# Two inverse square roots per round of an RWKV mixer, taken as exp(-ln/2) on ScalarE in place of a square root on ScalarE and a reciprocal on VectorE

## The reference, cut to what matters

```python
kk = hs(k * f('rwkv_k_k'))
kk = kk * lax.rsqrt(jnp.sum(kk * kk, axis=-1, keepdims=True) + 1e-12)
...
    decay = jnp.exp(-jnp.exp(w))
    a = jax.nn.sigmoid(f('rwkv_a0')[d] + xa @ f('rwkv_a_up')[d])
    yd, Sd = rwkv_scan(rh, hs(decay), kd, vh, kk, hs(a), s0[:, d], reverse=(d == 1))
...
y = ys[0] + ys[1]
mean = jnp.mean(y, axis=-1, keepdims=True)
var = jnp.mean(jnp.square(y - mean), axis=-1, keepdims=True)
yn = ((y - mean) * lax.rsqrt(var + GN_EPS)).reshape(b, n, D_RWKV) * f('rwkv_ln_g') + f('rwkv_ln_b')
out = (yn + (bonuses[0] + bonuses[1]).reshape(b, n, D_RWKV)) * g
```

## Time and profile before

| what | value |
|---|---|
| median of three runs | 3153.46 us (3147.15 to 3154.85) |
| the profiled execution | 3154.8 us |
| its span in the trace | 3153.0 us |
| busy: TensorE / weight loads | 2871.3 us (91%) / 2176.1 us (69%) |
| busy: VectorE / ScalarE / GpSimd | 1646.6 us (52%) / 1094.0 us (35%) / 165.9 us (5%) |
| mixer rounds, first layer | 364.2 to 688.3 us of the span |

### The profile page before, as it was taken

One profiled execution on the slowest core, in us unless ns is written; L12 is line 12 of the kernel. 1 busy time (PEld: TensorE's weight loads), 2 busy tenths in 40 slices (PEclk: granted clock), 3 DMA queues, 4 the chain that ended last, 5 costly groups with the idle time before them and its releaser, 6 DMA issues.

```text
span 3153.0 us, 48841 instructions
## 1 busy us (share of the span) xinstructions
PE 2871.3 (91%) x17315; PEld 2176.1 (69%) x17315; DVE 1646.6 (52%) x2172; ACT 1094.0 (35%) x1377; POOL 165.9 (5%) x209
## 2 busy tenths in 40 slices
PE   6899788889899999999878997888898999999997
PEld 1578555567688888888615785555677888888885
DVE  0466545444655555555515655555356555555554
ACT  0244322224344444444203443222234444444442
POOL 1000111110000000000010001111000000000000
PEclk9999988889899999999989998888898999999998
DMA  9765666645366666666496655666454666666662
GB/s 363 240 181 157 199 205 215 215 149 186 114 187 187 190 188 187 189 190 186 140 319 218 176 162 177 216 216 216 162 160 137 187 190 187 188 190 187 186 190 90
DMA packets 317241, 600.57 MB, mean 190 GB/s; under 512 B 23184, under 2 KB 29288, under 8 KB 316584
## 3 DMA queue, kind: packets, MB, share of 16 engines
q1 hardware_dynamic: 309488, 592.90, 59.3%
q10 hardware_dynamic: 7608, 5.60, 0.6%
HBM read 595.28 MB, written 3.15 MB: 190 GB/s over the span
## 4 chain that ended last, share of the span: by engine, by line
PE 76%; issue 10%; DVE 6%; DMA 5%; ACT 1%; POOL 1%; DVEq 1%; SPq 0%; ACTq 0%; POOLq 0%
PE bank L758 74%; DMA rawW<-in_w_ada 5%; PE bank L1110 1%; DVE xs L1291 1%; DVE AE L1495 0%; DVE ksq L1469 0%; DVEq L286 0%; SPq L335 0%; DVE BF L1495 0%; DVE tf L1272 0%; POOL qst L667 0%; DVE cs L1453 0%; DMA out_new_v<-proj 0%; PE bank L1042 0%; DVE x L1293 0%
## 5 line engine op out<-in xcount | busy, mean ns | idle before, releaser
L1219 DVE TENSOR_TENSOR loW<-rawW,hiW 128x1024 fp32r<-128x1024 f32 x592 | 724.9, 1226 | 737.0 <-ACT hiW L376 736.6
L376 ACT ACTIVATE hiW<-rawW 128x1024 fp32r<-128x1024 f32 x592 | 627.1, 1061 | 962.6 <-PE bank L758 960.6
L758 PE MATMUL bank<-hiW,actH 128*128 128x512 f32 (+1 forms) x2304 | 901.0, 391 | 18.3 <-DVE loW L1219 15.8
L758 PE MATMUL bank<-loW,actH 128*128 128x512 f32 (+1 forms) x2304 | 893.8, 388 | 0.0
L758 PE MATMUL bank<-hiW,actL 128*128 128x512 f32 (+1 forms) x2304 | 893.6, 388 | 0.0
L758 PEld LDWEIGHTS bank<-hiW,actH 128*128 128x128 f32 x2304 | 435.9, 189 | 109.0 <-DVE loW L1219 16.0
L758 PEld LDWEIGHTS bank<-hiW,actL 128*128 128x128 f32 x2304 | 435.3, 189 | 89.1
L758 PEld LDWEIGHTS bank<-loW,actH 128*128 128x128 f32 x2304 | 435.8, 189 | 87.8 <-issue 1.0
L758 PE MATMUL bank<-rawW,csR 128*32 128x512 f32 x1536 | 321.6, 684 | 107.5 <-DMA rawW<-in_w_ada 51.5
L758 PE MATMUL bank<-hiW,ffH 128*128 128x512 f32 x704 | 281.5, 400 | 3.2 <-DVE ffL L1589 3.2
L758 PE MATMUL bank<-hiW,ffL 128*128 128x512 f32 x704 | 280.9, 399 | 0.0
(11 more groups left out here) (246 smaller groups left out, 2264.4 us busy)
## 6 DMA issues: line engine op xcount, KB each, us to landing
rawW<-in_w_ada SPq DMA_DIRECT2D x384, 512.0 KB, 7.9
rawW<-in_w_gate SPq DMA_DIRECT2D x176, 512.0 KB, 3.7
rawW<-in_w_up SPq DMA_DIRECT2D x176, 512.0 KB, 3.7
rawW<-in_w_down SPq DMA_DIRECT2D x176, 512.0 KB, 3.6
rawW<-in_w_in SPq DMA_DIRECT2D x144, 512.0 KB, 3.6
rawW<-in_w_out SPq DMA_DIRECT2D x64, 512.0 KB, 3.6
rawW<-in_w_in SPq DMA_DIRECT2D x16, 160.0 KB, 2.3
x<-in_x_prompt SPq DMA_DIRECT2D x1, 1024.0 KB, 8.3
```

What stands on the lines that cost most here:

```text
L376: act.activation(hiW[:, c % LEAD, :, 0:width], rawW[:, c % SLOTS, :, 0:width], ACT.Copy).then_inc(hi_ready, 1)
L758: return pe.matmul(out, a, b, start=start, stop=stop, skip_group_check=True)
L1219: TT(loW[:, slot, :, 0:width], rawW[:, slot, :, 0:width], hiW[:, c % LEAD, :, 0:width].bitcast(F32), ALU.subtract).then_inc(lo_ready, 1)
```

## The change

The square root on ScalarE becomes a natural logarithm and, behind a new wait on ScalarE's own semaphore (`rw_ln`, `rw_vl`), an exponential with the scale -0.5. The result is then already the inverse square root, and the reciprocal on VectorE is left out. This is done at both places, and VectorE's count of steps per round falls by the two.

```diff
-VSTEPS, FSTEPS = 70, 27
+VSTEPS, FSTEPS = 70, 25
...
+        rw_ln, rw_vl = sem("rw_ln"), sem("rw_vl")
...
                     act.wait_ge(rw_ns, it + 1)
-                    act.activation(ksq[:], nrm[:], ACT.Sqrt).then_inc(rw_rs, 1)
+                    act.activation(ksq[:], nrm[:], ACT.Ln).then_inc(rw_ln, 1)
+                    act.wait_ge(rw_ln, it + 1)
+                    act.activation(ksq[:], ksq[:], ACT.Exp, scale=-0.5).then_inc(rw_rs, 1)
                     act.wait_ge(rw_VS, it + 1)
...
                     act.wait_ge(rw_vs, it + 1)
-                    act.activation(yy[3], yy[2], ACT.Sqrt).then_inc(rw_vr, 1)
+                    act.activation(yy[3], yy[2], ACT.Ln).then_inc(rw_vl, 1)
+                    act.wait_ge(rw_vl, it + 1)
+                    act.activation(yy[3], yy[3], ACT.Exp, scale=-0.5).then_inc(rw_vr, 1)
                     act.wait_ge(rw_o, it + 1)
...
                     dve.wait_ge(rw_rs, it + 1)
-                    R.step(dve.reciprocal(ksq[:], ksq[:]))
                     R.step(TT(kk[:], kk[:], ksq[:], ALU.mult))
...
                     dve.wait_ge(rw_vr, it + 1)
-                    R.step(dve.reciprocal(y3, y3))
                     R.step(TT(y0, y0, y3, ALU.mult))
```

## The result

Over twelve runs each, the changed kernel takes 3160.61 us (3153.76 to 3162.36) against 3153.79 us (3147.15 to 3158.2) before: ratio 1.0022, 95% interval 1.0014 to 1.0031. It is slower by 6.8 us, within the 0.3% that the prediction counts as no change, and three times its +2.0 us. The profiled execution took 3159.59 us, its span is 3157.8 us, 4.8 us more than before.

The account below looks back on a forecast made before the run. TensorE was taken as the bound, with KR waiting on both ksq's reciprocal path and the exponentials. Front +2.1 and end -0.1 gave +2.0 us: 3156.8 profiled, 3155.5 us predicted after allowing 1.3 us over the median; range 3146 to 3165 us.

Parts of the forecast that it names:

- The bound: Front of each round: ksq's reciprocal, 1.68 us, leaves the chain into KR; exponentials 0.07 us behind it take its place.
- Table loads: ScalarE, each round: six loads in place of five, for Copy, Sigmoid, Ln, Exp, Ln, Exp; none ahead of line 524.
- The price of 2.66 us per switch: ScalarE table switches: a drain besides the load, some +13 us in all, a slower kernel; chance 0.01.
- The logarithm: ScalarE's Ln at both places: taken as 0.42 us like the Sqrt, with bounds 0.36 and 0.83.
- Front: Round's front up to KR: exponentials end 0.33 us later, KR starts 0.26 us later; +2.1 us over eight rounds.
- End: Group norm at round's end: load and Exp replace the reciprocal, -0.04 us at two places; hidden at six other boundaries.
- One table: Rival, both places: one table serves Ln and Exp, no load between; -10.9 us, 3142.6 us; chance 0.08.
- Nothing else moves.: Rest of the round: head's load stays, mixF's copy goes 0.33 us later but is needed 10 us after; no transfers affected.
- The sum: Whole kernel: front +2.1 us and end -0.1 us give +2.0 us; forecast 3155.5 us, +0.06%, no difference.

Follow-up runs that it names:

- e3_one_table: The changed kernel with one hand-placed load of a table serving both Ln and Exp ahead of each round's first Ln; 3126.3 us, 0.9922 to the kernel before.

## Why the prediction was right, and where it was short

- **The bound.** Right: the reciprocal of ksq leaves the chain, the exponentials take its place, and VectorE idles 1.47 us ahead of KR (said: about 1.4).
- **Table loads.** Right: six per round, in the forecast order, each 1.283 us and 0.02 us from its neighbours, the load for Ln under way before nrm is ready. No drain shows between Ln and the next load. The price of 2.66 us per switch in the Trainium skill (ScalarE: Activation LUTs, "What ACT_TABLE_LOAD costs") does not hold in these rows.
- **The logarithm.** Unknown before; it takes 0.42 us, like the Sqrt.
- **Front.** +0.31 us for +0.26: the exponentials come 0.32 us later (said: 0.33), and KR starts 0.11 us behind the last one's end, where I had taken the 0.04 that it stood behind be.
- **End.** -0.06 us for -0.04, hidden at the other boundaries, as said.
- **One table.** It did not come by itself: the compiler did not choose that table. Placed by hand it confirmed the price part by part (0.97 for 1.03, 1.34 for 1.33), but not the total: 3142.6 us were worked out and 3126.3 measured, for the same reason as in the last point below. The statement that a set with both functions exists (Trainium skill, ScalarE: Activation LUTs, "Table sets: the hidden batching unit") is borne out by e3_one_table: one load a round serves logarithms and all exponentials.
- **"Nothing else moves."** This step failed. The sum moved everything behind KR by 0.26 us as one block. In fact the middle's length hangs on the clock that TensorE is granted in it, and by 0.3 us of lateness the rounds that were 2 us short went away. The sum's +2.0 is +2.4 of its own kind, and 4 us more come from the clock. That the time still fell within the range owes something to luck: the same effect, met from the other side, was worth 16 us in the one-table kernel. The sign was there to be read: cut at the Sigmoid's load, the rounds of the kernel before are 79.4 and 81.4 us long with the same instructions.

What stays open: what decides which rounds get a short low-clock stretch. The runs show that it is not monotonic in lateness (-1.24, -0.97, +0.42 and +1.25 us), and that the order of TensorE's work changes it too; no rule came out of them that would forecast the next kernel.

## What to carry to other kernels

Before you count what leaves a chain, ask what stands just behind it: here 1.7 us on VectorE were shadowed by a ScalarE path 0.07 us shorter, and the swap lengthened that one. Two functions that follow each other on ScalarE are worth the swap only if one table serves them, and you see in the trace whether the compiler chose it; placing the load by hand turned a loss of 0.2% into a gain of 0.8%, of which 10 of 26 us are the shorter paths and the rest the clock, which these runs give no way to plan. And where TensorE works at two clock levels in one phase, read the granted clock by round before you add up tenths of a microsecond: a repeated small delay can cost three times its length, or nothing.

## What the runs showed of the hardware that was not expected

Rounds of one kernel with the same instructions differ by up to 5.4 us, and the granted clock with them: 80.7 us at 0.85 and 75.4 us at 0.93 in the one-table kernel. Adding 1.25 us of waiting to each of eight rounds cost nothing measurable (0.9994), since three of six whole rounds came out at about 78.5 us and 0.91, and no middle stayed at 0.85.
